# Down products of the experts by high and low parts, four quarters of gate and up at a time

## What is computed

```python
def rms_norm(x, g):
    y = x * lax.rsqrt(jnp.mean(x * x, axis=-1, keepdims=True) + NORM_EPS)
    return y * g
def hierarchical_moe(xn, ...):
    t = xn.reshape(b * s, d)                       # 256 tokens, d = 2048
    g_val, g_idx = lax.top_k(softmax(t @ w_router_group + b_router_group), 1)
    ...                                            # top 2 of the group's 8 experts
    for grp in range(N_GROUPS):                    # 4 groups of 8 experts
        hid = silu(einsum('nd,edf->nef', t, w_e_gate[sl])) * einsum('nd,edf->nef', t, w_e_up[sl])
        out = out + einsum('nef,efd->nd', hid * combine[:, sl, None], w_e_down[sl])
    return out
def reference(...):
    h = x                                          # (1, 256, 2048) float32
    xn = rms_norm(h, norm_mix_g)
    proj = xn @ w_in + b_in                        # q, k, v, and two gating halves
    y_a = sliding_window_sink_attention(q, k, v, attn_sinks)
    y_b = chunked_spatial_gating(u_sgu, v_sgu, norm_v_g, w_spatial, b_spatial)
    merged = g_a * (y_a @ w_branch_a) + g_b * (y_b @ w_branch_b)
    h = h + merged @ w_out
    h = h + hierarchical_moe(rms_norm(h, norm_ffn_g), ...)
    return rms_norm(h, norm_final_g)
```

## Time and profile before

| | us |
|---|---|
| median of 3 runs (1138.86 to 1139.37) | 1139.13 |
| the profiled execution | 1139.23 |
| its span in the trace | 1137.5 |
| expert phase, first quarter to last down product | 597 to 1122 |

### The profile page before, as it was taken

How to read it: one execution, slowest core, us unless ns; L and a number is a source line. 1 busy time by engine, 2 the same in 40 slices (tenths; PEclk the granted TensorE clock), 3 DMA queues, 4 the chain that set the end, 5 groups by cost and what they waited for, 6 DMA issues and landing times.

```text
span 1137.5 us, 13564 instructions
## 1 busy us (share of the span) xinstructions
PE 1106.9 (97%) x4884; PEld 719.6 (63%) x4884; DVE 508.0 (45%) x720; ACT 403.1 (35%) x546; POOL 2.7 (0%) x13
## 2 busy tenths in 40 slices
PE   7999999999999999999979999999999999999995
PEld 6888888788888888888864344634455443644343
DVE  5546555575464554746663222432225222332225
ACT  5335555653433334444331222222232222312224
POOL 0000000000000000000000000000000000000000
PEclk8999999999999999999989999999999999999998
DMA  9554445468666566577538999999999999989962
GB/s 321 197 194 158 157 157 175 163 234 271 204 211 203 184 210 197 171 255 250 191 114 280 407 412 413 350 331 414 414 412 304 350 413 415 369 297 402 413 253 112
DMA packets 105883, 312.12 MB, mean 274 GB/s; under 512 B 13128, under 2 KB 14192, under 8 KB 97136
## 3 DMA queue, kind: packets, MB, share of 16 engines
q1 hardware_dynamic: 105840, 311.54, 74.8%
HBM read 309.41 MB, written 2.10 MB: 274 GB/s over the span
## 4 chain that ended last, share of the span: by engine, by line
PE 92%; DVE 3%; ACT 3%; issue 1%; DMA 0%; DVEq 0%; SPq 0%; ACTq 0%
PE bank L1733 20%; PE bank L1470 18%; PE bank L1471 17%; PE bank L1472 17%; PE bank L1753 10%; PE bank L1782 3%; PE bank L1742 1%; PE bank L1572 1%; PE bank L1674 1%; PE bank L1596 1%; PE bank L1477 1%; PE bank L1793 1%; ACT whi L592 1%; DVE wlo L902 1%; PE bank L1811 1%
## 5 line engine op out<-in xcount | busy, mean ns | idle before, releaser
L902 DVE TENSOR_TENSOR wlo<-raw,whi 128x2048 fp32r<-128x2048 f32 x92 | 210.7, 2291 | 201.1 <-ACT whi L592 201.1
L592 ACT ACTIVATE whi<-raw 128x2048 fp32r<-128x2048 f32 x92 | 176.2, 1916 | 254.6 <-PE bank L1472 254.6
L1733 PE MATMUL bank<-slot,xe 128*64 128x512 f32 x1024 | 247.5, 605 | 0.0
L1470 PE MATMUL bank<-whi,actT_hi 128*128 128x512 f32 x608 | 240.9, 396 | 2.2 <-DVE wlo L902 1.3
L1472 PE MATMUL bank<-wlo,actT_hi 128*128 128x512 f32 x608 | 237.7, 391 | 0.0
L1471 PE MATMUL bank<-whi,actT_lo 128*128 128x512 f32 x608 | 237.7, 391 | 0.0
L1733 PEld LDWEIGHTS bank<-slot,xe 128*64 128x64 f32 x1024 | 62.3, 136 | 133.3 <-issue 129.7
L1470 PEld LDWEIGHTS bank<-whi,actT_hi 128*128 128x128 f32 x608 | 114.7, 189 | 28.6 <-DVE wlo L902 2.9
L1472 PEld LDWEIGHTS bank<-wlo,actT_hi 128*128 128x128 f32 x608 | 114.6, 188 | 24.3
L1471 PEld LDWEIGHTS bank<-whi,actT_lo 128*128 128x128 f32 x608 | 114.7, 189 | 22.8
L1753 PE MATMUL bank<-slot,hT 128*128 128x512 f32 x256 | 125.7, 614 | 0.4 <-ACT hT L819 0.4
(11 more groups left out here) (228 smaller groups left out, 1003.1 us busy)
## 6 DMA issues: line engine op xcount, KB each, us to landing
slot<-in_w_e_gate SPq DMA_DIRECT2D x128, 512.0 KB, 8.7
slot<-in_w_e_up SPq DMA_DIRECT2D x128, 512.0 KB, 10.2
slot<-in_w_e_down SPq DMA_DIRECT2D x64, 1024.0 KB, 10.6
raw<-in_w_gate SPq DMA_DIRECT2D x64, 512.0 KB, 4.4
raw<-in_w_in SPq DMA_DIRECT2D x56, 512.0 KB, 4.7
raw<-in_w_out SPq DMA_DIRECT2D x32, 512.0 KB, 4.8
raw<-in_w_branch_a SPq DMA_DIRECT2D x16, 512.0 KB, 4.7
raw<-in_w_branch_b SPq DMA_DIRECT2D x16, 512.0 KB, 4.4
```

The lines of the kernel that those rows point to most:

```text
L592: return act.activation(whi[slot][:], src, ACT.Copy)
L902: dve.tensor_tensor(wlo[s][:], raw[:, k, :], whi[s][:], ALU.subtract).then_inc(lo_made, 1)
L1470: pe.matmul(o, x_hi, w_hi, start=start, stop=False)
L1733: mm = pe.matmul(dst[h * CAP:(h + 1) * CAP, :], xe[:, kt, r, :], w[:, :, k, :], start=kt < 2, stop=kt >= KT - 2)
```

## The change

The down weights leave the ring: the ring has 8 slots for quarters of gate and up, and `down` has two slots, one for each load `f`. Both halves of down are now multiplied by parts: `down_0` is gone, `down_t` does 24 fp32r matmuls for an expert, and `d_hi`, `d_lo` exist twice, in memory that was slots 8 and 9. `hT_0` is gone, `hT_hi` and `hT_lo` hold both halves.

PE's order: the four quarters of an expert together, then all of down of the preceding one, then `turn_hidden`. In a group's first two experts it is quarters of 0, scatters (or `gather_weights` and `count_left`), quarters of 1, scatters, `turn_hidden(0)`, `down_t(0)`, `turn_hidden(1)`. At a group's end the gather of the next is one piece ahead of the last `down_t`, and `gather_weights` follows it. DVE spreads its additions over the first expert's steps. SP loads four quarters of expert `j` and then the down weights of `j - 1`, each down load behind the wait for `d_lo` of `j - 2`.

```diff
-RING = 12
+RING, DOWN_RING = 8, 2
...
-                for q, kb in enumerate((144, 152, 160, 168, 96, 104, 112, 120, 32, 40, 80, 88))]
-        d_hi = at("d_hi", 16, [P, PIECE], F32R)
-        d_lo = at("d_lo", 24, [P, PIECE], F32R)
+                for q, kb in enumerate((144, 152, 160, 168, 96, 104, 112, 120))]
+        down = [at(f"down{f}", kb, [P, PIECE]) for f, kb in enumerate((80, 88))]
+        d_hi = [at(f"d_hi{f}", kb, [P, PIECE], F32R) for f, kb in enumerate((16, 32))]
+        d_lo = [at(f"d_lo{f}", kb, [P, PIECE], F32R) for f, kb in enumerate((24, 40))]
...
-        hT_0 = at("hT_0", 186.5, [P, P])
-        hT_hi = at("hT_hi", 187, [P, P], F32R)
-        hT_lo = at("hT_lo", 187.5, [P, P], F32R)
+        hT_hi = at("hT_hi", 186.5, [P, 2, P], F32R)
+        hT_lo = at("hT_lo", 202, [P, 2, P], F32R)
...
-                n = down_at(j, f) % RING
-                sp.dma_start(slot[n][:], wd_v[e + j, :, f, :]).then_inc(slot_in[n], 16)
+                sp.dma_start(down[f][:], wd_v[e + j, :, f, :]).then_inc(down_in[f], 16)
...
-            load_down(0, 0, 0)
+            load_gate_up(1, 2, 0)
             after_raw(3)
-            load_gate_up(1, 2, 0)
-            await_used(sp, DENSE - 2)
             load_gate_up(1, 3, 0)
             await_used(sp, DENSE - 1)
+            load_down(0, 0, 0)
             load_down(0, 1, 0)
-            load_gate_up(2, 0, 0)
-            load_gate_up(2, 1, 0)
...
-            def after_down(i, j, f):
-
-                sp.wait_ge((d0_used, d_lo_made)[f], EPG * i + j + 1)
...
-                for j in range(3, EPG):
-                    after_gate_up(i, j - 2, 0)
-                    load_gate_up(j, 0, e)
-                    after_gate_up(i, j - 2, 1)
-                    load_gate_up(j, 1, e)
-                    after_down(i, j - 3, 0)
-                    load_down(j - 1, 0, e)
-                    after_gate_up(i, j - 2, 2)
-                    load_gate_up(j, 2, e)
-                    after_gate_up(i, j - 2, 3)
-                    load_gate_up(j, 3, e)
-                    after_down(i, j - 3, 1)
-                    load_down(j - 1, 1, e)
...
+            def load_expert(i, j, e):
+
+                for k4 in range(4):
+                    if j < 2:
+                        after_gate_up(i - 1, EPG - 2 + j, k4)
+                    else:
+                        after_gate_up(i, j - 2, k4)
+                    load_gate_up(j, k4, e)
+                if j:
+                    for f in range(2):
+                        if j == 1:
+                            after_parts(i - 1, EPG - 1, f)
+                        else:
+                            after_parts(i, j - 2, f)
+                        load_down(j - 1, f, e)
+
+            def load_last(i, e):
                 for f in range(2):
-                    after_gate_up(i, EPG - 2, f)
+                    after_parts(i, EPG - 2, f)
                     load_down(EPG - 1, f, e)
...
-            def down_hi(i, j):
+            def down_hi(i, j, f):
 
                 if j:
-                    act.wait_ge(d1_used, EPG * i + j)
+                    act.wait_ge(d_used, down_count(i, j - 1, f) + 1)
                 elif not (isinstance(i, int) and i == 0):
-                    act.wait_ge(scat_full, 8 * i)
-                n = down_at(j, 1)
-                act.wait_ge(slot_in[n % RING], arrived(i, n))
-                act.activation(d_hi[:], slot[n % RING][:], ACT.Copy).then_inc(d_hi_made, 1)
+                    if f == 0:
+                        act.wait_ge(scat_full, 8 * i)
+                    act.wait_ge(d_used, down_count(i - 1, EPG - 1, f) + 1)
+                act.wait_ge(down_in[f], 16 * EPG * i + 16 * j + 16)
+                act.activation(d_hi[f][:], down[f][:], ACT.Copy).then_inc(d_hi_made, 1)
...
-                act.activation(hT_0[:], bank[j % 2][:, 0:P], ACT.Copy).then_inc(hT_made, 1)
-                if j:
-                    act.wait_ge(d1_used, EPG * i + j)
-                act.activation(hT_hi[:], bank[j % 2][:, P:2 * P], ACT.Copy).then_inc(hT_made, 1)
+                act.activation(hT_hi[:], bank[j % 2][:, 0:2 * P].rearrange("p (a b) -> p a b", a=2),
+                               ACT.Copy).then_inc(hT_made, 1)
...
                 for j in range(EPG - 1):
                     gate_low(i, j)
                     silu(i, j)
+                    hidden_turned(i, j)
+                    down_hi(i, j, 0)
+                    down_hi(i, j, 1)
                     if j == 1:
                         act.wait_ge(selT_full, i + 1)
                         act.activation(selT[:], bank[6][:, 0:T], ACT.Copy).then_inc(selT_made, 1)
-                    hidden_turned(i, j)
-                    down_hi(i, j)
                 last = EPG - 1
                 gate_low(i, last)
+                silu(i, last)
+                hidden_turned(i, last)
                 if another_follows:
                     gathered_a(i + 1, 0)
-                silu(i, last)
+                    gathered_a(i + 1, 2)
+                    gathered_a(i + 1, 4)
+                down_hi(i, last, 0)
                 if another_follows:
-                    gathered_a(i + 1, 2)
-                hidden_turned(i, last)
-                down_hi(i, last)
-                if another_follows:
-                    gathered_a(i + 1, 4)
                     gathered_a(i + 1, 6)
-                else:
+                down_hi(i, last, 1)
+                if not another_follows:
                     output_hi(i)
...
+            def down_lo(i, j, f):
+                dve.wait_ge(d_hi_made, down_count(i, j, f) + 1)
+                dve.tensor_tensor(d_lo[f][:], down[f][:], d_hi[f][:], ALU.subtract).then_inc(d_lo_made, 1)
...
-                for j in range(EPG - 1):
+                gate_sum(i, 0)
+                if after_another:
+                    add(i - 1, range(1, 3), SCATTER)
+                hidden(i, 0)
+                if after_another:
+                    add(i - 1, range(3, 8), SCATTER)
+                hidden_lo(i, 0)
+                down_lo(i, 0, 0)
+                down_lo(i, 0, 1)
+                for j in range(1, EPG - 1):
                     gate_sum(i, j)
                     hidden(i, j)
+                    hidden_lo(i, j)
+                    down_lo(i, j, 0)
+                    down_lo(i, j, 1)
                     if j == 1 and another_follows:
                         dve.wait_ge(selT_full, i + 1)
                         pick(i + 1)
                         pick_pairs(i + 1)
-                    hidden_lo(i, j)
-                    down_lo(i, j)
                 last = EPG - 1
                 gate_sum(i, last)
+                hidden(i, last)
+                hidden_lo(i, last)
                 if another_follows:
-                    gathered_v(i + 1, 1)
-                hidden(i, last)
-                if another_follows:
-                    gathered_v(i + 1, 3)
...
-                down_lo(i, last)
-                if another_follows:
-                    gathered_v(i + 1, 5)
-                    gathered_v(i + 1, 7)
-                else:
+                    for q in range(1, KT // 2, 2):
+                        gathered_v(i + 1, q)
+                down_lo(i, last, 0)
+                down_lo(i, last, 1)
...
-                if k4 == 0 and j > 1:
-                    pe.wait_ge(hT_made, 2 * EPG * i + 2 * j - 2)
-                    pe.wait_ge(hT_lo_made, EPG * i + j - 1)
-                elif k4 == 0 and not (isinstance(i, int) and i == 0):
-                    pe.wait_ge(hT_made, 2 * EPG * i + 2 * j - 2)
+                if k4 == 0 and not (isinstance(i, int) and i == 0 and j < 2):
                     pe.wait_ge(hT_lo_made, EPG * i + j - 1)
...
-            def down_1(i, j, blocks):
-
-                if blocks[0] == 0:
-                    pe.wait_ge(hT_lo_made, EPG * i + j + 1)
-                    pe.wait_ge(d_lo_made, EPG * i + j + 1)
-                last = j == EPG - 1
-                for b in blocks:
-                    cols = slice(b * COLS, (b + 1) * COLS)
-                    mm = three(bank[2 + b][:], hT_hi[:], hT_lo[:], d_hi[:, cols], d_lo[:, cols], False, last)
...
+            def down_t(i, j):
+                pe.wait_ge(hT_lo_made, EPG * i + j + 1)
+                for f in range(2):
+                    pe.wait_ge(d_lo_made, down_count(i, j, f) + 1)
+                    last = j == EPG - 1 and f == 1
+                    for b in range(NC):
+                        cols = slice(b * COLS, (b + 1) * COLS)
+                        mm = three(bank[2 + b][:], hT_hi[:, f, :], hT_lo[:, f, :], d_hi[f][:, cols], d_lo[f][:, cols],
+                                   j == 0 and f == 0, last)
+                        if last and b < 3:
+                            mm.then_inc(o_full, 1)
+                    mm.then_inc(d_used, 1)
 
             def gather(i, qs):
 
@@ -1812,62 +1764,44 @@
                     pe.matmul(bank[dst][:], selT[:, tok], o_lo[:, cols], start=False, stop=True).then_inc(scat_full, 1)
```

(62 more changed lines are left out.)

106 lines of the change are left out of this document (24 added, 82 removed).

## The result

| | us |
|---|---|
| before, median of 4 runs (1138.86 to 1139.99) | 1139.25 |
| after, median of 4 runs (1157.40 to 1160.41) | 1159.41 |
| ratio, with its 95% interval | 1.0174 (1.0156 to 1.0192) |
| the profiled execution after (span 1158.7) | 1160.41 |

A forecast was written before the change was run, and what follows sets the result against it. TensorE bounds, memory a per cent behind. By differences, -41.3 + 4 x 4.6 + 3 x 3.0 + (4.6 - 0.7) + 4 x 2.8 = +1.2; the walk gave +1.6, so 1140.8, plus 5 for the clock: 1146 us, range 1133 to 1156.

The forecast's parts named there:

- the landing of the loads: End of each group's backlog of loads: 2.3 us on top of 81.0 us of transfer at 414 GB/s.
- Products: Per expert on TensorE, fp32r products replace f32 matmuls: 13.62 us against 14.91, 41.3 us saved for 32 experts.
- A: Before `down_t(0)` in all four groups: TensorE stands 4.6 us while the hT copy, `d_hi` and `d_lo` run.
- B: Before `down_t(7)` at three group ends: `down_lo(7, 0)` queued behind VectorE's gather copies, TensorE waits 3.0 us.
- C: Before the last expert's down in the last group: TensorE waits 4.6 us for copy, `d_hi` and `d_lo`.
- The queue of loads: SP's loads stand behind expert 1's down loads: 90.4 us from A to end of `down_t(6)`, memory 2.8 late per group.
- The clock: Half-rate stretches after TensorE's waits: 2 us per fall, A's free, C 2, B three times 1, together +5 us.
- Rival 3: The clock costs more: every B falls at 3.8, C at 4, A's falls exceed their cover; 1161 us, chance 0.12.
- Rival 1: The memory keeps up, SP's late issue costs nothing and the saved products come through; 1131 us, chance 0.16.
- rival 2: The clock holds through the waits, so the sum stands at 1141 us, no change; chance 0.20.
- Rival 4: All stalls hidden and the loads early, needing `d_hi` ahead of `hidden_turned` on ScalarE; 1098 us, chance 0.02.

The follow-up runs named there:

- early_hi_first: Changed kernel, with the first `d_hi` and `d_lo` of each group's first expert made ahead of the waits for turned `hid`, o_hi/o_lo sharing the second half's memory: 1142.60 us.
- early_hi_last: Changed kernel, with the first `d_hi` of each group's last expert made before the wait for turned `hid`, its `d_lo` before VectorE's gather copies: 1144.65 us.
- fill_a: Changed kernel with 15 idle matmuls put into TensorE's wait before the first down of each group only: 1161.59 us.
- gu3_first: Changed kernel with SP issuing expert 3's four quarters ahead of expert 1's down loads, which then come with those of expert 2: 1150.85 us.
- fill_all: Changed kernel with idle matmuls in TensorE's waits before the down parts: a group's first and last, the very last, and experts 4 to 6: 1146.61 us.
- early_both: Changed kernel with the edits of early_hi_first and early_hi_last together, SP's order of loads unchanged: 1135.04 us, ratio 0.9965 to the kernel before.
- best_fill: early_both with quarter and down loads interleaved on SP, plus idle matmuls in waits at down of experts 1 and 6 and at the very end: 1128.53 us.

## Why the prediction was wrong in its size

Two terms failed, by nearly the same amount: the number of clock falls, put at 5 us and worth 14.3, and the landing of the loads, for which the four groups took 9.9 us more than the sum gave them. A third error went the other way and hid 4.6 us of this.

**Products: right.** An expert in mid-group takes 13.13 us (13.62 predicted), TensorE is busy 24.9 us less in spite of the half-rate stretches, and fp32r products start 0.23 apart. One term was mis-sized in the kernel's favour: four quarters in a row take 7.01 us, not 4 x 1.87 = 7.48, and the 1.87 of the earlier trace rows were read between other products. Why a lone quarter takes longer stays open: it isn't the change between f32 and fp32r alone, since the quarter at 655.48 stands between two f32 pieces (the turning and `down_0`) and takes 1.87 too. What all its neighbours there have in common is that they fill 128 places where the quarter's products fill 64; no run isolates that. Twice 0.47 us is 0.9 at the first A, and 2.9 of the 3.8 at the three group ends (the other 0.9 is small terms, such as the turning, 0.36 for 0.55); in the memory's stretch it gave nothing.

**Stalls A, B, C: right.** A 4.60 to 4.69 (4.6), B 3.07, 2.98, 2.98 (3.0), C 4.69 (4.6), each in its place and ended by `d_lo`. early_hi_first and early_hi_last, which take only these away, return 16.8 and 14.8 us, in both cases with the falls at B.

**The queue of loads: right in its mechanism, 2.5 us per group too small.** A to the turning of expert 7 was put at 90.4; with the clock held it is 92.9 (371.50 / 4). The step that failed is the landing: 83.3 us after A (81.0 + 2.3) in the sum, 85.85 in after (85.75, 84.53 and 85.44 in the other groups), where ScalarE takes up the last half at 707.00:

```profile
704.56 1.91 ACT L748 ACTIVATE d_hi<-down 128x2048 fp32r<-128x2048 f32 x1 [4.20 <-DMA down<-in_w_e_down]
707.00 1.91 ACT L748 ACTIVATE d_hi<-down 128x2048 fp32r<-128x2048 f32 x1 [0.54 <-DMA down<-in_w_e_down]
```

The rates place the 2.5 us, but for 0.1. Against 414 GB/s all through, 1.5 us are lost in the first three us behind A, before the loads run at full rate, and 2.0 at the end, where from 704.5 the rate is 180 GB/s and less until 707.0: 3.5 in all, for which the sum had 2.3. The other 1.2 are the sag from 628 to 632, for which it had nothing. The other groups have the same three parts (1.5, 0.9 to 1.0, and 1.0 to 2.1). Since the two halves land 2.4 us apart, `down_t(6)` starts only at 708.94 and its 5.6 us end at 714.5 at full clock, where the sum, with half of it behind the last `d_lo`, gives 714.0 for the same landing. And since TensorE's own work in the stretch is less than 87.6 with quarters at 7.01, memory is late by some 8 us per group and not by 2.8: 84.7 (5.6 + 0.85 + 5 x 13.13 + 7.01 + 5.6) against 92.9. The products' gain was lost here, as the prediction said, more of it than it said.

**The clock: the number of falls failed.** It was put at 5 us and cost 14.3 in the profiled execution, 12.8 by the medians. Three parts:
- B was counted at half of three falls of 2 us, 3 us. All three fell and cost 5.7. The rule of the Trainium skill that the prediction weighed (TensorE: Matmul & The Clock Gate, section "Why this matters for your kernels") said that all of B falls, and the trace of after agrees. No more than that: four traces have B's waits of 3.0 us unchanged (after, fill_a, gu3_first, early_hi_first), and 8 of their 12 were followed by half-rate products, so in the count the prediction's half was not far off, and that all three fell in after may be chance. C cost 2.8 instead of 2.
- The waits for late loads were foreseen as waits ("1 to 2 us before `down_t(5)` or `down_t(6)`"), and no fall was set for them. Of eight waits of 1.8 to 2.2 us six were followed by half-rate products. Before `down_t(6)` no cover is left: three falls at 1.6 us each, about the 4.5 us between after and fill_all in the second row of the account (the three groups lose 1.7, 1.8 and 1.3, the second gains 0.4).
- 1.3 us for the fall ahead of the first A.
A fall's own price was well chosen: 1.4 to 2.9 us where uncovered, within the bounds 0 and 4. The number of falls was not. That those at A cost nothing was right, as fill_a shows.

In sum, the profiled execution is 14.6 later than 1145.8, which the forecast had rounded up to 1146: 9.3 the clock (14.3 for 5), 9.9 the memory's stretch, and -4.6 at the first A and the group ends (3.8 of it the quarters).

**The rivals.** Rival 3 (1161) came nearest in time. Its sum was another, though: falls at A that exceed their cover, which they don't. Rival 1 fell (the DMA engines do run dry, the backlog is not delivered in time); rival 2 fell (15 stretches at half rate in the expert phase). Rival 4 named its condition, `d_hi` ahead of `hidden_turned`. early_both meets that and lands at 1135, not 1098, because the 1098 forgot the loads: a group's 50.33 MB at 414 GB/s take 121.6 us, against 133.6 that a group took before. At that rate no order of TensorE's work can bring more than 12 us per group. best_fill's second and third groups take 131.2.

What stays open: why the rate sags 8 to 10 us behind each A with the DMA engines busy, why the same wait of 3.0 us is followed by a fall in one trace and not in another, and how near to 121.6 an order of loads can come. A third down slot, which would take the wait for `d_lo` off the head of the queue, wasn't tried.

## What to carry to other kernels

A cheaper product pays only until the next resource: divide the bytes of a stage by the measured rate first, and put that floor beside the engine's sum before counting the gain. When work is moved so that no long piece lies between a producer and its user, put the producer ahead of what else its engine does there; two such swaps turned +1.7% into -0.4% here, a part of it because the falls of the clock at B and C (8.5 us in after) went with the waits. In a queue that issues in order, a load with a wait sets the time of all that stand behind it, so place it by when its wait ends; and once the engines never run dry, stop reordering.

## What the runs showed of the hardware

- The same wait of 3.0 us (B) was followed by half-rate products in 8 of 12 cases: three of three in after and in fill_a, two of three in gu3_first, none of three in early_hi_first. Waits of about 2 us in dense work were followed by them in six of eight cases (after); in the same trace waits up to 0.78 us between dense products never were. Behind thin products (`gather_weights`) a wait of 0.71 us was followed by them in seven of thirteen traces.
- A fall is worth what lies behind it: 1.4 to 2.9 us where TensorE sets the time, nothing in front of late loads. Fifteen idle products in a wait of 4.7 us held the clock at 1.00 and did not delay what followed (5.31 us from the turning to the first product of down in fill_a, 5.40 in after).
- Behind a dry stretch the loads were above 400 GB/s within three us. In all four groups of after they sagged to between 209 and 258 GB/s in the ninth and tenth us behind A, with a DMA share of 0.81 to 1.03, and were at 410 or more again in the twelfth.
- Four f32 quarters in a row took 7.01 us; standing singly between other products, f32 or fp32r, four times 1.87, or 7.48.
